# Seven block products in place of eight for a third row pair in the first chunk pair of an output product

## What is computed

```python
y_conv = conformer_conv_branch(u_conv, conv_w, conv_b, conv_ln_g, conv_ln_b, w_conv_out)
y_mla = mla_branch(c_q, c_kv, k_pe, cos, sin, q_norm_g, w_uq, kv_norm_g, w_ukv, w_mla_out)
gates = jax.nn.sigmoid(gate_logits + b_gate).reshape(B, S, N_BRANCH, D)
merged = gates[:, :, 0, :] * y_conv + gates[:, :, 1, :] * y_mla
x = x + merged @ w_out
x = x + memory_cross_attention(rms_norm(x, norm_mem_g), rms_norm(mem, mem_norm_g), w_xq, w_xkv, w_xo)
x = x + squared_relu_mlp(rms_norm(x, norm_ffn_g), w_ff1, w_ff2)
```

## Time and profile before

| | |
|---|---|
| median of 3 runs | 1596.12 us (1596.04 to 1596.23) |
| the profiled execution's own time | 1596.36 us |
| its span | 1594.1 us |
| TensorE matmul busy | 1582.9 us, 99% |
| VectorE busy | 1299.3 us, 82% |
| ScalarE busy | 900.2 us, 56% |
| loads | 336.68 MB, mean 211 GB/s |
| granted TensorE clock, mean | 0.998 |

### The profile page before, as it was taken

How to read it: one execution, slowest core, us unless ns; L and a number is a source line. 1 busy time by engine, 2 the same in 40 slices (tenths; PEclk the granted TensorE clock), 3 DMA queues, 4 the chain that set the end, 5 groups by cost and what they waited for, 6 DMA issues and landing times.

```text
span 1594.1 us, 22178 instructions
## 1 busy us (share of the span) xinstructions
PE 1582.9 (99%) x7915; PEld 1343.4 (84%) x7915; DVE 1299.3 (82%) x1741; ACT 900.2 (56%) x1133; POOL 94.5 (6%) x174
## 2 busy tenths in 40 slices
PE   9999999999999999999999999999999999999997
PEld 8888888888888888888888888888888888888886
DVE  5588999999998998786887787886779676968687
ACT  6444456555555556754566666455655565546655
POOL 6500010000000000000000000000000000000001
PEclk9999999999999999999999999999999999999999
DMA  7666655655555666657664676888678867987694
GB/s 254 203 187 186 194 158 178 174 181 172 182 177 174 209 200 185 197 177 249 212 195 145 179 230 186 279 258 291 181 256 267 266 217 219 286 259 237 207 293 147
DMA packets 169581, 336.68 MB, mean 211 GB/s; under 512 B 10377, under 2 KB 23297, under 8 KB 169089
## 3 DMA queue, kind: packets, MB, share of 16 engines
q1 hardware_dynamic: 164608, 324.84, 64.4%
q0 software_dynamic: 4864, 10.80, 3.1%
q10 hardware_dynamic: 32, 0.01, 0.0%
HBM read 326.16 MB, written 2.10 MB: 206 GB/s over the span
## 4 chain that ended last, share of the span: by engine, by line
PE 98%; DVE 0%; ACT 0%; issue 0%; ACTq 0%; POOL 0%; POOLq 0%; DVEq 0%
PE ps L2508 15%; PE ps L1937 12%; PE ps L1939 12%; PE ps L1938 12%; PE ps L2217 9%; PE ps L2215 9%; PE ps L2216 9%; PE ps L2510 7%; PE ps L1950 1%; PE ps L2126 1%; PE ps L2335 1%; PE ps L2121 1%; PE ps L2104 1%; PE ps L2106 1%; PE ps L2105 1%; PE ps L2160 1%
## 5 line engine op out<-in xcount | busy, mean ns | idle before, releaser
L695 ACT ACTIVATE w_both<-raw 128x1024 fp32r<-128x1024 f32 x524 | 553.2, 1059 | 498.7 <-PE ps L1939 178.5
L1188 DVE TENSOR_TENSOR w_both<-raw,w_both 128x1024 fp32r<-128x1024 f32 x524 | 637.3, 1222 | 201.6 <-ACT w_both L695 199.9
L2508 PE MATMUL ps<-a_both,w_both 128*128 128x512 f32 x1024 | 321.6, 395 | 0.0
L1937 PE MATMUL ps<-w_both,a_both 128*128 128x512 f32 (+1 forms) x636 | 251.4, 395 | 0.1
L1939 PE MATMUL ps<-w_both,a_both 128*128 128x512 f32 (+1 forms) x636 | 247.1, 388 | 0.0
L1938 PE MATMUL ps<-w_both,a_both 128*128 128x512 f32 (+1 forms) x636 | 246.9, 388 | 0.0
L2510 PEld LDWEIGHTS ps<-a_both,w_both 128*128 128x128 f32 x1024 | 192.4, 188 | 45.4
L1249 DVE SCALAR_TENSOR_TENSOR acc<-hconv,cwk,acc 128x256 f32<-128x256 f32 x464 | 201.1, 486 | 7.7 <-PE ps L2160 7.6
L2510 PE MATMUL ps<-a_both,w_both 128*128 128x256 f32 x1024 | 201.2, 278 | 0.0
L2215 PE MATMUL ps<-w_both,c_hi 128*128 128x512 f32 x414 | 161.4, 390 | 0.0
L2216 PE MATMUL ps<-w_both,c_hi 128*128 128x512 f32 x414 | 161.1, 389 | 0.0
(11 more groups left out here) (418 smaller groups left out, 2208.4 us busy)
## 6 DMA issues: line engine op xcount, KB each, us to landing
raw<-in_w_ff_dram SPq DMA_DIRECT2D x225, 512.0 KB, 4.6
raw<-in_w_in_dram SPq DMA_DIRECT2D x137, 512.0 KB, 4.2
t_raw<-in_w_ff_dram SPq DMA_DIRECT2D x31, 1024.0 KB, 7.2
raw<-in_w_mla_out_dram SPq DMA_DIRECT2D x32, 512.0 KB, 4.3
raw<-in_w_conv_out_dram SPq DMA_DIRECT2D x32, 512.0 KB, 4.5
raw<-in_w_out_dram SPq DMA_DIRECT2D x32, 512.0 KB, 4.4
raw<-in_w_ukv_dram SPq DMA_DIRECT2D x16, 512.0 KB, 3.8
raw<-in_w_xkv_dram SPq DMA_DIRECT2D x16, 512.0 KB, 3.8
```

What stands on the lines that cost most here:

```text
L695: act.activation(whi[:, s, :], raw[:, s, :], ACT.Copy).then_inc(hi_ready, 1)
L1188: dve.tensor_tensor(wlo[:, s, :], raw[:, s, :], whi[:, s, :].bitcast(F32), ALU.subtract).then_inc(lo_ready, 1)
L1937: pe.matmul(sum_, x_hi[:, k0 + k, tok], w_hi, start=(first and k == 0), stop=False)
L2508: pe.matmul(both, whi[:, s, cols[n]], a_both[:, :, k0 + k, :], start=(first and k == 0), stop=False)
```

## The change

The first chunk pair (p = 0) gets its own order and positions, in which three row pairs (row blocks 0 to 5) take seven products. The second chunk pair keeps the old ones. Its core:

```diff
+OUT_ORDER = ((0, 6), (0, 8), (1, 6), (1, 8), (0, 0), (1, 0), (0, 10), (1, 10), (0, 2),
+             (1, 2), (0, 12), (0, 4), (1, 4), (0, 14), (1, 12), (1, 14))
+OUT_LEFT, OUT_RIGHT = (4, 8, 11), (5, 9, 12)
+OUT_WS_HIGH = (2, 6, 10)
+OUT_WS_LOW = {2: (0, 1), 3: (0, 0), 6: (1, 1), 7: (1, 0), 10: (2, 1), 11: (2, 0)}
+OUT_PLANS = ((OUT_ORDER, OUT_LEFT, OUT_RIGHT, OUT_WS_HIGH, OUT_WS_LOW),
+             (FF2_ORDER, LEFT, RIGHT, (5, 10), {5: (0, 1), 6: (0, 0), 10: (1, 1), 11: (1, 0)}))
...
             for p in range(2):
-                for i, (c, k) in enumerate(FF2_ORDER):
+                for i, (c, k) in enumerate(OUT_PLANS[p][0]):
...
+                    if c == 2 and k == 7:
+                        act.wait_ge(h3_made, 5)
+                        act.activation(h3_hi[:], h3_sum[:], ACT.Copy).then_inc(h3_hi_ready, 1)
...
-                chunk_squares(sq_res, xres[:, :, NC * c:NC * (c + 1)], c, SS_MEM + TT * c)
+                chunk_squares(sq_out, xres[:, :, NC * c:NC * (c + 1)], c, SS_MEM + TT * c)
...
+            def h3_sums():
+
+                dve.wait_ge(turn_hi, 2 * (T_MRG + 1) + 1)
+                x11, x12, x21, x22 = (ps[:, 6, SEQ * k + P * t:SEQ * k + P * (t + 1)] for t, k in ((0, 0), (0, 1), (1, 0), (1, 1)))
+                s1, s2, s3, s4 = (h3_sum[:, i, :] for i in range(4))
+                dve.tensor_copy(s4, x21).then_inc(h3_made, 1)
+                dve.wait_ge(h3_made, 1)
+                dve.tensor_tensor(s1, s4, x22, ALU.add).then_inc(h3_made, 1)
+                dve.tensor_tensor(s3, x11, s4, ALU.subtract).then_inc(h3_made, 1)
+                dve.wait_ge(h3_made, 3)
+                dve.tensor_tensor(s2, s1, x11, ALU.subtract).then_inc(h3_made, 1)
+                dve.wait_ge(h3_made, 4)
+                dve.tensor_tensor(s4, x12, s2, ALU.subtract).then_inc(h3_made, 1)
...
+                    if (c, k) == (2, 6):
+                        h3_sums()
...
+                    if (c, k) == (3, 1):
+                        dve.wait_ge(h3_hi_ready, 1)
+                        dve.tensor_tensor(h3_lo[:], h3_sum[:], h3_hi[:].bitcast(F32), ALU.subtract).then_inc(h3_lo_ready, 1)
...
-                    if k in (5, 6):
-                        ws_low(OUT, p, 0, 6 - k)
-                    if k in (10, 11):
-                        ws_low(OUT, p, 1, 11 - k)
+                    if k in sum_low:
+                        ws_low(OUT, p, *sum_low[k])
...
+                        if m == 2:
+                            pe.wait_ge(h3_lo_ready, 1)
```

More of the change, by code:

```diff
@@ L974, in out_squares @@
                 act.wait_ge(mixed, 3 * (c // 2 + 2))
-                chunk_squares(sq_res, xres[:, :, NC * c:NC * (c + 1)], c, SS_MEM + TT * c)
-            for p in range(2):
+                chunk_squares(sq_out, xres[:, :, NC * c:NC * (c + 1)], c, SS_MEM + TT * c)
+            for p, (_, _, right, sum_high, _) in enumerate(OUT_PLANS):
                 for k in range(FF2_UNITS):
@@ L980, in _ @@
                         y_out(OUT, p, 0)
-                    if k + LEAD in RIGHT:
+                    if k + LEAD in right:
                         hi_second(U_WOUT + FF2_UNITS * p + k + LEAD, 0)
@@ L1631, in add_chunk @@
                 dve.tensor_tensor(cols, ps[:, bank:bank + 2, :], cols, ALU.add).then_inc(chunk_out, 1)
-            for p in range(2):
+            for p, (_, left, right, _, sum_low) in enumerate(OUT_PLANS):
                 u = U_WOUT + FF2_UNITS * p
@@ L1636, in _ @@
                     i = k + LEAD
-                    if i in LEFT:
+                    if i in left:
                         dve.wait_ge(chunk_out, N_WOUT + 2 * p)
-                        w_sums(OUT, p, LEFT.index(i), u)
-                    if i in RIGHT:
+                        w_sums(OUT, p, left.index(i), u, left_at=left)
+                    if i in right:
                         lo_second(u + i, 0)
@@ L2217, in product, with seven_pair @@
                 return pe.matmul(ps[:, bank, :], x_lo, w_hi, start=False, stop=last, skip_group_check=True)
-            def seven_pair(g, p, u, r, banks, first_use, between, sums, b=late, x_hi=c_hi, x_lo=c_lo):
+            def seven_pair(g, p, u, r, banks, first_use, between, sums, b=late, x_hi=c_hi, x_lo=c_lo, plan=(FF2_ORDER, LEFT, RIGHT)):
+                order, left, right = plan
+                end = len(left) - 1
                 def hidden(k, t):
@@ L2236, in seven_pair @@
                 begun = set()
-                for i, (c, k) in enumerate(FF2_ORDER):
+                for i, (c, k) in enumerate(order):
                     pe.wait_ge(lo_ready, u + i + 1 + r)
                     first_use(i, k)
[L2240 to L2243, removed]
+                    if i in left:
+                        m = left.index(i)
+                        mm = product(ONES_BANK, *hidden(2 * m, 0), *slot(i, 0), first=(m == 0), last=(m == end))
+                        if m == end:
                             mm.then_inc(y_step, 1)
                         product(banks[0], *hidden(2 * m + 1, 0), *slot(i, 1)).then_inc(used, 1)
-                    elif i in RIGHT:
-                        m = RIGHT.index(i)
+                    elif i in right:
+                        m = right.index(i)
                         pe.wait_ge(h_lo_ready, sums)
+                        if m == 2:
+                            pe.wait_ge(h3_lo_ready, 1)
                         product(banks[1], *combined(3, m), *slot(i, 1), first=banks[1] not in begun).then_inc(used, 1)
@@ L2253, in seven_pair @@
                             for t in range(TT):
-                                ends = n == 1 and (i == 15 or (i == LEFT[1] + 2 and t == 0))
+                                ends = n == 1 and (i == 15 or (i == left[end] + 2 and t == 0))
                                 mm = product(banks[c] + t, *hidden(k + n, t), *slot(i, n), first=banks[c] + t not in begun, last=ends)
@@ L2303, in _ @@
             for p in range(2):
+                plan = OUT_PLANS[p][:3]
                 def out_waits(i, k):
@@ L2309, in out_waits @@
                         pe.wait_ge(chunk_out, N_WOUT + 2 * p - 1 + i // 2)
-                    if i == LEFT[0]:
+                    if i == plan[1][0]:
                         pe.wait_ge(mixed, 3 * (p + 1))
```

57 lines of the change are left out of this document (34 added, 23 removed).

## The result

The changed kernel takes 1600.78 us, the median of ten runs (1599.24 to 1601.35); the kernel before takes 1596.17 us on the same chip (ten runs, 1595.77 to 1596.48). The ratio is 1.0027, with a 95% interval of 1.0017 to 1.0036. The change makes the kernel slower, by 4.6 us at the median and by 3.2 us or 5.0 us in a single run, for the ten runs fall into two groups: four from 1599.24 to 1599.55 (middle 1599.4), at a mean granted clock of 0.998, and six from 1600.56 to 1601.35 (middle 1601.2), at 0.997 but for one at 0.998. The forecast of 1599.3 is the lower group.

The account below looks back on a forecast made before the run. TensorE was taken to bound the kernel: three pauses of 3.71 to 3.87 us behind VectorE, less 0.68 gained, plus about 0.1 for a load, gave 3.2 us on 1596.12: 1599.3 us, range 1597.5 to 1600.9.

Parts of the forecast that it names:

- Bound and gain: TensorE, busy 99% of the span, sets the time; one block product of three matmuls goes, gaining 0.68 us.
- the third pause: TensorE's wait at unit 11 of the first chunk pair for VectorE's low part: 2.26 to 2.42 us.
- Work added on VectorE: In the first chunk pair, one more set of weight sums and its split, less a saving: 4.33 us more.
- the walk: VectorE's instructions followed from 767.31 in the changed order: TensorE pauses at units 8, 10, 11, 3.03 to 3.19 us slower net.
- the three low parts: VectorE's `lo` of units 8, 10 and 11, predicted to begin at 773.38, 776.51 and 781.49 to 781.65.
- the restart of 0.17: TensorE resumes 0.17 us after the VectorE instruction it waited for, counted in each pause.
- The load of unit 12: Needed by the third weight sums; lands 778.2 to 780.1, adding nothing to 1.2 us, about 0.1 at the middle.
- the third sums: VectorE's third set of weight sums in the first chunk pair, predicted to start between 778.90 and 779.06.
- Edits at nothing: Activation sums, ScalarE's copy and splits, reordered loads and similar edits hide and cost nothing; up to 2.8 us without cover.
- The clock, rival 4: TensorE's clock drops from 1.00 to 0.50 in the pause at unit 11: 1602 us or above. Chance 0.03.
- The range: The 8 in 10 range for the whole kernel's time: from 1597.5 to 1600.9 us.

Follow-up runs that it names:

- two: Changed kernel without the third row pair (third sums of weights and their products gone, third activation sums still made): median 1597.68 us, ratio 1.0009.
- spread: Changed kernel with all three row pairs kept but placed evenly, LEFT units 3, 8, 12 in place of 4, 8, 11: median 1596.57 us, ratio 1.0003.
- again_b: Changed kernel, unchanged, the second of three single profiled runs: 1600.08 us.
- again_c: Changed kernel, unchanged, the third of three single profiled runs: 1600.89 us.
- again: Changed kernel, run once more unchanged: median 1599.44 us of 11 runs, ratio 1.0024.
- pause2: Kernel before, with VectorE making the low part of unit 11 two extra times in the first chunk pair: median 1598.25 us, ratio 1.0012.

## Why the prediction was right, and where it wasn't

- **Bound and gain.** Right: three matmuls went, and behind the third pause the pace holds: 81 matmuls in 801.33 - 782.83 = 18.50 us, 0.228 each, the first of them longer. One word of the working is wrong: the 126 matmuls from 769.65 to 798.21 are those of units 5 to 15 with eight extra products, not twelve; the number and the pace hold.
- **Work added on VectorE, and the walk.** Right to 0.12 us at each of the three low parts. The pauses of 0.36, 1.09 and 2.26 to 2.42 came as 0.35, 1.05 and 2.41 by the starts of the matmuls, the restart of 0.17 included, and the chunk pair ended at 801.33, predicted 801.24 to 801.40. The net of 3.12 us is the sum of the pauses, 3.81, less the product saved, 0.68. `two` has the first two pauses alone and is 1.6 us slower; `spread` has nearly none and keeps the product saved, and all but 0.5 us of the loss is gone.
- **The load of unit 12.** Right: the third sums wait 0.21 us for it, at 778.97. It is not the long end of the earlier trace rows that came. The figures that the prediction takes from the Trainium skill, DMA: Bandwidth & Descriptors, stand there in the section Anatomy of one DMA — SWDGE (gpsimd) path, on copies issued by GpSimd, and these loads are issued by SyncE, so the shortest load of the earlier trace rows, 3.6 us, neither bears these figures out nor refutes them.
- **Edits at nothing.** Right, and none shows in the result. The five instructions of 128x128 take 0.28 to 0.29 us each, where I took 0.28; they push the split from 730.06 to 731.44, and TensorE is busy without a break from 728 to 766. VectorE's timeline of the changed kernel, and that stretch (length, busy times with TensorE first, clock, DMA share, GB/s):

```profile
730.06 0.29 DVE L1544 COPY h_sum<-ps 128x128 f32<-128x128 f32 x1 [1.41 <-ACT c_hi L732]
...
731.44 1.28 DVE L1230 TENSOR_TENSOR c_lo<-ps,c_hi 128x512 fp32r<-128x512 f32 x2
```

```profile
728.00:766.00 38.00, 38.00 (x178) 31.57 (x177) 28.41 (x32) 17.91 (x20) 0.00 (x0) 1.00 0.69 235
```

- **The clock, rival 4.** This is the step that failed, in its chance and in its size, as far as the upper group is this rival. "Chance 0.03", and "I put it at 1602 or above". Of 24 runs of the changed kernel in all, 12 are in the lower group (1599.02 to 1599.66), 11 in the upper (1600.56 to 1601.42) and one, `again_b`, between them with the clock at 1.00. So the chance was about 0.45 and the price 1.6 to 1.8 us, not 2.7 or more. The chance rested on one row, in which TensorE stopped within 1584 to 1586 and the clock was 0.50 only in 1588 to 1590; one stop at the end of the kernel doesn't say how short a pause can be and still have a fall in some runs. And I priced the lower level to the end of the chunk pair, where it held for 3.4 us (`again_c`). The Trainium skill, TensorE: Matmul & The Clock Gate, section Why this matters for your kernels, warns of idle gaps between bursts of matmuls, but of longer ones than the changed kernel has; its runs differ from it. Here a pause of the matmuls of 2.0 to 2.1 us, with two shorter ones in the 9 us before it, had the drop in nearly half of the runs by their times, and one of 2.7 us alone in five of seven.
- **The range.** That it held the median, 1600.78, at its upper end was luck: that end was set for another reason (loads near their long end, which did not come), and the median of ten runs in two groups fell where it did by how many came into each. In `again` it was 1599.44. Two values, 1599.3 and 1600.9 to 1601.2, with about even chances, would have been the forecast.

What stays open: why an execution falls into the one group or the other, and what made the single runs of `pause2` (1600.38), `spread` (1598.15) and of the kernel before (two of 15 at 1597.6, one of 29 at 1597.24) later than the rest. Of these, the run of `spread` and the one at 1597.24 list a mean clock of 0.997 too, without a pause above 0.8 us in this chunk pair in the profiles of those kernels, so this mean alone is a weak sign of a drop. Waits at the start of the kernel, as the 0.8 us of `again_b`, are another way for a single run to be late; none of these runs was profiled. Nor was it tried whether the two shorter pauses ahead of the third have a part in the drop: no run has a pause of 2.1 us by itself.

## What to carry to other kernels

Before a sum of work is added to an engine that is second to the bound, walk that engine's timeline from its last wait, instruction by instruction, beside the times at which the bound engine takes the units: the cover is what is left at the tightest unit (1 us here), not the nominal lead of three. Price a pause of TensorE from start to start of its matmuls, and by the clock: one recorded as 1.6 us of idle time cost 1.9, and one of 2 us or more may cost 1.6 us on top. The two shorter pauses of `two` had no slower group in 11 runs; whether the same pause in several pieces is cheaper than in one was not tried. Where a saving is smaller than the work it puts on a nearly full engine (0.68 us on TensorE against 5.4 on VectorE here), the saving is easily lost: the best order found, 1596.57 us, is not told apart from the kernel before.

## What the runs showed of the hardware

- TensorE's granted clock fell from 1.00 to 0.50 in or right behind a pause of 2.0 to 3.9 us, in a part of the runs that grew with the pause: by the times, one of 11 runs at most at 1.6 us, 11 of 24 at 2.0 to 2.1 us with two shorter pauses ahead, five of seven at 2.7 us, all five at 3.9 us; three profiles show it. It held for about 3.4 us in two profiles and 6.8 us in the third, and 128x512 matmuls were then 0.43 us apart, 1.9 times the 0.2267 of the upper level.
- A VectorE and a GpSimd instruction of 128x512 that each read two tiles from SBUF held each other up: 1.78 and 2.19 us, where they take 0.68 and 1.3 alone.
- Behind a pause that VectorE ended, TensorE was back at its pace 0.16 to 0.17 us later than the end of VectorE's instruction, its first matmul recorded with 0.50 us in place of 0.39.
- A VectorE instruction of 128x128 that reads PSUM takes 0.28 to 0.29 us, against 0.41 for 128x256.
